# Decay and beta rows of a gated-delta mixer by transposes of broadcast columns, with the rate sums one tile earlier

## The reference

```python
bc = chunks_s(beta)
gc = jnp.cumsum(chunks_s(g), axis=-1)          # g: log decay of a token and head
diff = gc[..., :, None] - gc[..., None, :]
decay = jnp.where(lower, jnp.exp(jnp.where(lower, diff, 0.0)), 0.0)
kb = kc * bc[..., None]
a_mat = jnp.where(strict, jnp.einsum('nbhid,nbhjd->nbhij', kb, kc) * decay, 0.0)
t_inv = lax.linalg.triangular_solve(eye + a_mat, ..., lower=True, unit_diagonal=True)
attn_intra = jnp.where(lower, jnp.einsum('nbhid,nbhjd->nbhij', qc, kc) * decay, 0.0)
```

## Time and profile before

| | |
|---|---|
| median of 3 runs | 1611.51 us (1609.36 to 1613.82) |
| span of the profiled execution | 1606.7 us |
| own time of the profiled execution | not recorded; the median less the span is 4.8 us |
| PE busy | 1312.8 us, 82% of the span |
| DVE / ACT / POOL busy | 598.5 / 435.9 / 213.8 us |
| bytes moved | 528.42 MB, mean 329 GB/s |

### The profile page before, as it was taken

How to read it: one execution, slowest core, us unless ns; L and a number is a source line. 1 busy time by engine, 2 the same in 40 slices (tenths; PEclk the granted TensorE clock), 3 DMA queues, 4 the chain that set the end, 5 groups by cost and what they waited for, 6 DMA issues and landing times.

```text
span 1606.7 us, 21602 instructions
## 1 busy us (share of the span) xinstructions
PE 1312.8 (82%) x9392; PEld 856.4 (53%) x9392; DVE 598.5 (37%) x1159; ACT 435.9 (27%) x645; POOL 213.8 (13%) x119
## 2 busy tenths in 40 slices
PE   7999999999999987766657758999886775675677
PEld 3787798999999832212212215998521221221226
DVE  4788547885387201001101104785210110110116
ACT  4564455444454210000000003683200000000005
POOL 0224244886400100000000000000000000000000
PEclk9999999999999998777877879999988777877889
DMA  9425543444648999999999999459899999999992
GB/s 400 172 89 230 211 174 144 172 177 145 241 154 344 374 425 428 427 427 427 426 429 427 425 422 382 173 213 381 359 427 425 426 429 426 428 427 427 427 409 106
DMA packets 52624, 528.42 MB, mean 329 GB/s; under 512 B 4784, under 2 KB 4912, under 8 KB 20144
## 3 DMA queue, kind: packets, MB, share of 16 engines
q1 hardware_dynamic: 51952, 525.22, 79.8%
q10 hardware_dynamic: 576, 1.79, 0.3%
HBM read 525.94 MB, written 1.05 MB: 328 GB/s over the span
## 4 chain that ended last, share of the span: by engine, by line
PE 52%; DMA 38%; SPq 3%; DVE 2%; ACT 2%; issue 1%; POOL 0%; DVEq 0%; ACTq 0%
PE bank L672 25%; PE bank L1294 9%; DMA ring<-in_w_up 8%; DMA ring<-in_w_down 7%; DMA work<-in_w_gate 7%; DMA ring<-in_w_gate 6%; DMA work<-in_w_up 4%; DMA work<-in_w_down 4%; PE bank L1314 3%; SPq L566 3%; PE bank L1376 3%; PE bank L665 2%; DMA ring<-in_dense 2%; PE bank L1444 2%; PE bank L914 1%; PE bank L786 1%
## 5 line engine op out<-in xcount | busy, mean ns | idle before, releaser
L1294 PE MATMUL bank<-ring,work 128*32 128x512 f32 x1232 | 319.0, 730 | 135.3 <-DMA ring<-in_w_up 69.8
L672 PE MATMUL bank<-work_rounded,ring_rounded 128*128 128x256 f32 (+1 forms) x2000 | 301.8, 286 | 2.2 <-DVE work_rounded L2099 1.3
L672 PEld LDWEIGHTS bank<-work_rounded,ring_rounded 128*128 128x128 f32 x2000 | 265.9, 188 | 9.4 <-issue 2.9
L672 PE MATMUL bank<-xn_rounded,ring_rounded 128*128 128x256 f32 (+1 forms) x1472 | 248.9, 285 | 1.2 <-DVE xn_rounded L2140 1.2
L1294 PEld LDWEIGHTS bank<-ring,work 128*32 128x32 f32 x1232 | 69.8, 130 | 308.6 <-issue 114.9
L2725 DVE TENSOR_TENSOR work<-work,bank 128x512 f32<-128x512 f32 x16 | 11.0, 688 | 547.0 <-PE bank L1294 547.0
L672 PEld LDWEIGHTS bank<-xn_rounded,ring_rounded 128*128 128x128 f32 x1472 | 202.6, 188 | 5.4 <-issue 2.7
L1294 PE MATMUL bank<-work 128*32 128x512 f32 x496 | 157.6, 677 | 34.5 <-DMA work<-in_w_gate 19.1
L1988 POOL TENSOR_TENSOR ring_rounded<-ring,ring_rounded 128x2048 fp32r<-128x2048 f32 (+1 forms) x35 | 149.2, 4279 | 158.9 <-ACT ring_rounded L1517 158.9
L1517 ACT ACTIVATE ring_rounded<-ring 128x2048 fp32r<-128x2048 f32 (+1 forms) x76 | 133.1, 1797 | 47.2 <-PE bank L672 28.5
L1314 PE MATMUL bank<-ring,work 128*32 128x512 f32 x576 | 123.0, 650 | 16.7 <-DMA ring<-in_w_down 16.7
(11 more groups left out here) (351 smaller groups left out, 1685.3 us busy)
## 6 DMA issues: line engine op xcount, KB each, us to landing
ring<-in_dense SPq DMA_DIRECT2D x47, 2048.0 KB, 8.4
ring<-in_w_up SPq DMA_DIRECT2D x38, 2048.0 KB, 30.2
ring<-in_w_gate SPq DMA_DIRECT2D x36, 2048.0 KB, 29.5
ring<-in_w_down SPq DMA_DIRECT2D x34, 2048.0 KB, 29.3
work<-in_w_gate SPq DMA_DIRECT2D x16, 2048.0 KB, 23.1
work<-in_w_down SPq DMA_DIRECT2D x16, 2048.0 KB, 32.2
spare<-in_w_gate SPq DMA_DIRECT2D x8, 2048.0 KB, 29.0
work<-in_w_up SPq DMA_DIRECT2D x8, 2048.0 KB, 31.9
```

Source lines behind the costliest of these rows:

```text
L672: last = mm(out, rv(high_store[r][:, at:at + P]), rv(x[part][k]), start=opens and k == 0 and j == 0, stop=closes and k == n_k - 1 and j == 2)
L1294: ins = mm(out[slots(y), :], xg[:, k, slots(y)], expert_columns(w, at, 512), start=k == 0, stop=k == KT - 1)
```

## The change

1. The three rate sums move ahead of the fourth value tile (i = 3), into bank 3 instead of bank 7. VectorE takes them out of PSUM between the convolutions of value tiles 2 and 3 instead of after both.
2. Decay rows are no longer products of rates and a triangle: the cumulative column `gcol`, which VectorE has copied already, is broadcast to 128 columns and transposed on TensorE. Beta rows are made in the same way from beta's column. There are 32 + 16 such products a program, and as many transposes.
3. The wait for gate_cols 2 moves ahead of `decay_rows(0)`, since its input is now `gcol`.

```diff
@@ -890,7 +890,18 @@
             if b == 0:
                 sums_qk(0)
                 sums_qk(1)
+        def rate_sums():
+
+            pe.wait_ge(S["gate_cols"], 1)
+            released(pe, USE["v"] + 1)
+            rates = glog.rearrange("p u c -> p (u c)")
+            for i, m in enumerate((cums[0], cums[1], ones)):
+                last = mm(bank[3][:, 32 * i:32 * i + 32], m, rates, start=True, stop=True)
+            signal(last, "rate_mm")
+
         for i in range(4):
+            if i == 3:
+                rate_sums()
             dense_split(USE["v"] + i, [(FIRST["w_in"] + 2, i)], both)
             if i in (1, 2):
                 sums_qk(2 * i)
@@ -921,32 +932,31 @@
         def query_products(u, b):
             signal(heads(bank[b], lambda h: kc[:, h, 1, columns_of(u)], lambda h: qc[:, h, columns_of(u)]), "qk_mm")
 
+        def spread(out, columns):
+
+            for h in range(HEADS):
+                last = nc.tensor.transpose(out[:, P * h:P * h + P], columns[:, h:h + 1].to_broadcast([P, P]), ident)
+            return last
+
         def decay_rows(e):
             d, u = e % 2, token_of(e // 2, e % 2)
-            b = bank[row_bank[e]]
-            signal(heads(b, lambda h: glog[:, u, 4 * d + h:4 * d + h + 1].to_broadcast([P, P]), lambda h: cums[d]), "g_rows")
+            signal(spread(bank[row_bank[e]], gcol[:, d, u]), "g_rows")
 
         def beta_rows(e):
             u = token_of(e // 2, 0)
             pe.wait_ge(S["g_diff"], e + 1)
             if e >= 4:
                 pe.wait_ge(S["qd_exp"], e - 3)
-            b = bank[row_bank[e]]
-            signal(heads(b, lambda h: beta[:, u, h:h + 1].to_broadcast([P, P]), lambda h: ident), "b_rows")
+            signal(spread(bank[row_bank[e]], beta[:, u, 0:HEADS]), "b_rows")
 
         row_bank = (6, 0, 7, 1, 6, 3, 7, 0)
-        pe.wait_ge(S["gate_cols"], 1)
         pe.wait_ge(S["qk_norm"], 6)
-        rates = glog.rearrange("p u c -> p (u c)")
-        for i, m in enumerate((cums[0], cums[1], ones)):
-            last = mm(bank[7][:, 32 * i:32 * i + 32], m, rates, start=True, stop=True)
-        signal(last, "rate_mm")
+        pe.wait_ge(S["gate_cols"], 2)
         decay_rows(0)
         released(pe, USE["v"] + 2)
         decay_rows(1)
         key_products(0, 4)
         key_products(1, 5)
-        pe.wait_ge(S["gate_cols"], 2)
         decay_rows(2)
         beta_rows(0)
         released(pe, USE["v"] + 3)
@@ -2329,21 +2339,20 @@
         weights_low(FIRST["w_in"] + 3)
         norm_qk(4)
         norm_qk(5)
-        for i in (2, 3):
-            conv_all("v", vc, i, 8)
-
         shape = [P, HEADS, P]
 
         def by_head(b):
             return b[:].rearrange("p (h t) -> p h t", h=HEADS)
 
+        conv_all("v", vc, 2, 8)
         dve.wait_ge(S["rate_mm"], 3)
-        both_rates = [bank[7][:, 32 * i:32 * i + 32].rearrange("p (u d h) -> p d u h", u=4, d=2) for i in range(3)]
+        both_rates = [bank[3][:, 32 * i:32 * i + 32].rearrange("p (u d h) -> p d u h", u=4, d=2) for i in range(3)]
         for d in range(2):
             v.tensor_copy(gcol[:, d], both_rates[d][:, d])
         after(v.tensor_copy(gtot, both_rates[2]))
         signal(v.tensor_tensor(gdiff, gtot, gcol, ALU.subtract), "gate_cols")
         dve.wait_ge(S["gate_cols"], 2)
+        conv_all("v", vc, 3, 8)
         row_bank, key_bank = (6, 0, 7, 1, 6, 3, 7, 0), (4, 5, 4, 5)
 
         def difference(e):
```

## The result

The changed kernel takes 1615.3 us, the median of 20 runs (1608.9 to 1624.8); the kernel before, run beside it, takes 1611.4 (20 runs, 1607.9 to 1616.6). The ratio is 1.0021, with a 95% interval from 1.0011 to 1.0030: slower by some 3.4 us. That is less than the 0.3% that the prediction called no change, but it is not the 0.2 us of the forecast. By the ratio the time is 1611.5 x 1.0021 = 1614.9, at the upper edge of the range. The interval lies clear of 1. A second set of runs of the same kernel (e9) gave 1.0026 (1.0013 to 1.0039).

A forecast was written before the change was run, and what follows sets the result against it. The prediction took a chain over ScalarE, VectorE and GpSimd, not TensorE, to bound the stretch; +0.59 for the rate sums and -0.43 for beta_rows(6) gave +0.16 us, so 1611.5 + 0.2 = 1611.7 us, range 1609 to 1615.

The forecast's parts named there:

- no change: Whole kernel: differences within about 0.3%, 4.8 us, can't be told from none; chance 0.88 of landing there.
- rival of the whole saving: Stretch bound by TensorE, so all 5.8 us saved there would show: 1605.7 us; chance 0.05.
- the step sum: Chain to z's second half: rate sums ahead of the fourth value tile +0.59, shorter beta_rows(6) -0.43, together +0.16 us.
- The 4.8 us: Whole kernel: the median of the runs lies 4.8 us above the profiled span and moves with it.
- The earlier wait for `gate_cols`: Ahead of decay_rows(0): VectorE's copies end about 102.55, TensorE comes at 103.34, so 0.8 us of room.
- the clock: z behind the hole ahead of beta_rows(6): low clock for 3.4 us loses 1.7 us, 1613.4; chance 0.25, through z 0.04.
- The rule on transposes: Around the two holes: transposes don't count as busy TensorE, so they lengthen the holes and make 1613.4 us likely.
- Its lasting through all of z: Low clock over all 5.66 us of z's second half, twice the time there: 1617.4 us; chance 0.04.
- the 0.16 passes on: Behind z, up to the solved blocks at 172.28: the chain is almost all TensorE, so the 0.16 us delay remains.

The follow-up runs named there:

- e9: The changed kernel as it is, run again beside the kernel before: 1613.7 us, ratio 1.0026.
- e2: Changed kernel plus six unused 512-column products in TensorE's holes ahead of beta_rows(4) and beta_rows(6), against the kernel before: 1612.4 us, ratio 1.0018.
- e10: Changed kernel plus 24 unused 128-column products (96 instructions) in the two holes, against the kernel before: 1609.7 us, ratio 0.9997.
- e11: Changed kernel plus 48 unused fp32 transposes (96 instructions) in the two holes, against the kernel before: 1609.8 us, ratio 0.9998.
- e4: Kernel before with only the rate sums and their copies moved ahead, rows still by fp32 products, against the kernel before: 1612.0 us, ratio 1.0001.
- e5: Changed kernel plus 24 tiny real products (96 instructions) ahead of the fifth key step, against the kernel before: 1613.7 us, ratio 1.0024.
- after: The profiled execution of the changed kernel: 1612.37 us, span 1610.5 against 1606.7 for the kernel before.
- e1: Changed kernel plus 96 empty TensorE instructions in its first idle time, against the kernel before: 1613.9 us, ratio 1.0019.
- e8: Kernel before with only the beta rows by transposes, plus 8 tiny products for the 32 instructions saved, against the kernel before: 1610.9 us, ratio 1.0003.
- e6: Kernel before plus 40 tiny real products (160 instructions) ahead of the fifth key step, against the kernel before: 1616.3 us, ratio 1.0043.
- e3: Changed kernel plus six unused 512-column products in the two holes and 72 empty instructions, against the kernel before: 1613.6 us, ratio 1.0020.

## Why the prediction was right or wrong

**Right: what bounds the stretch.** 5.8 us less work on TensorE brought nothing, since the chain runs over ScalarE, VectorE and GpSimd there. The rival of the whole saving (0.05) is out.

**Right: the step sum.** Forecast were L1517 later by 0.59, the first exponential's reader at 109.81, `beta_rows(6)` at 124.67 and z's second half 0.16 later, at 125.12. Measured were 0.56, 109.77, 124.60 and 124.98, which is 0.02 later; with the holes filled z's end moved by +0.09 (e2), -0.05 (e10) and -0.14 us (e11). Transposes are 0.109 us apart (forecast 0.1125), also with a broadcast column as their stationary, which no row had shown. The 4.8 us that the prediction put between span and median were no constant: 1.8 are, and 3.0 were a fast profiled execution; for the forecast of a difference this didn't matter. The earlier wait for `gate_cols` cost nothing: 103.13 is directly behind the tile.

**Wrong by its chance: the clock.** The mechanism stood among the rivals, with its place (z behind the hole) and its price of 1.7 us; measured were 1.53. It was given 0.29 in all, against which stood that a hole of 1.62 us had left the clock full. That was evidence for 1.62 us and no more: holes of 2.28 (e4), 2.48 (e5), 2.38 to 2.41 (after, e9, e1) and 2.97 us (e8) all lost it over z. The prediction itself had put the hole ahead of `beta_rows(6)` at some 4 us. At full clock that is right (e10: 3.74 us of fillers and 0.36 of idle); in the changed kernel the first hole's fall stretched the key products, and 2.41 were left. So a hole 2.5 times as long as the one it relied on was its own number, and 0.29 was too little. The rule on transposes that it weighed beside it named the right outcome by a reason that e11 refutes: the idle time did it, not the transposes. Its lasting through all of z did not happen.

**Not foreseen: the instruction stream.** "Behind z the chain is TensorE almost throughout [...], so the 0.16 passes on" is the sentence that failed. 1.5 us are added at the 32x32 burst, 55 us behind `beta_rows(6)`, by what the change does to the count of instructions: 96 fewer, so that two edges of the stream lie in one burst. The counts at e6, e5 (count restored: no stall), e6 (count raised in the kernel before: stall) and e10 (count restored at no cost) show this; e2 shows that the clock has no part in its start. No term or rival of the prediction had it.

**The sum.** In the profile 0.02 + 1.53 + 1.54 = 3.1 us stand behind the burst, near the 3.4 us of the ratio. Either cause removed alone did not show in the timed runs (e2 1.0018; e5 1.0024 with its own 1.4 us), both removed did (e10 0.9997). How the 3.4 us of the timed runs divide between the two is open: in e2 the stall brought a fall of the clock of its own, and in e4, e5 and e10 the fall that the kernel before has at 187 us was missing (1.3 us), in e5 and e10 with one near 246 to 249 us instead (1.7 us). The prices don't simply add, and one profile a kernel doesn't say how often each fall comes. Open too is the 0.7 us that the changed kernel lost in the expert layers, which varied from profile to profile (in e9 it was 0.3 us won).

The range of 1609 to 1615 held only by the ratio (1614.9; the median of the changed kernel's own runs lies at 1615.3). That it held is luck in part: half of the loss had no term in the prediction, and the other half was a rival. It is no change by the bound of 0.3%, but a loss that 20 runs do tell from nothing, and twenty times the 0.16 us of the step sum.

## What to carry to other kernels

Work taken off an engine beside the critical path becomes idle time; on TensorE ask where it collects and what stands right behind it, because a full clock may depend on it, and unused work in the hole can be the cheaper thing to have there. An edit that changes the number of instructions moves every later edge of the instruction stream against the program; where two edges come to lie in one dense burst, the engine can stall. Where a dense burst of short instructions shows a new "issue" gap far behind the edit, count the records up to it in several versions, and compare with a version of the same count before blaming the edit. Padding for such a comparison has to be real instructions in a place where the engine waits anyway.

## What the runs showed of the hardware

- A hole of 1.62 us left TensorE's granted clock full in its profile (1.63 us in e6 too); every hole of 2.12 to 2.97 us ahead of the beta rows lost it (two each in after, e9, e1 and e5, one each in e4 and e8), for some 3.4 us each time.
- fp32 transposes kept the clock as products did (e11 beside e10: 1.00 from 95 to 135 us in both).
- An fp32 transpose takes one product record and one weight load, 0.109 us apart, an fp32 product of 128 columns two of each and 0.234 us.
- TensorE's instruction stream has an edge every 256 instructions. Two edges 1.4 us apart, in a burst of 32x32 products, stalled it by 1.4 to 2.0 us of idle time; edges 3.2 us apart cost 0 to 0.3 us. Empty instructions moved no edge (e1).
- The stall can itself lose the clock: 1.5 to 1.6 us more in e1, e2 and e3, some 6 us in e6, nothing in after and e9.
